# A streaming encoder layer whose product operands are laid out on 64-byte starts

## What is computed

```python
proj = rmsnorm(x) @ w_in                        # 1024 -> 4096: x_a | x_b | g_a | g_b
y_a  = rg_lru(causal_conv4(x_a))                # gates by 8 blocks of 128 x 128
y_b  = (pool(x_b) - x_b) @ w_g * scale          # 4 groups of 256, windows 2, 4, 8, 16
x = x + (sig(g_a) * (y_a @ w_br_a) + sig(g_b) * (y_b @ w_br_b)) @ w_out
gu = rmsnorm(x) @ w_gu                          # 1024 -> 2 x 2816
x = x + (silu(gu[:, :2816]) * gu[:, 2816:]) @ w_down
y = rmsnorm(x)                                  # final norm
```

## Time and profile before

| | |
|---|---|
| median of three runs | 2699.14 us |
| the profiled execution: its time | 2699.44 us |
| its span, first to last instruction | 2697.6 us |
| TensorE busy (matmul) | 2680.8 us, 15422 instructions |
| VectorE busy | 2053.7 us |
| ScalarE busy | 1359.4 us |
| GpSimd busy | 197.0 us |
| moved by DMA | 486.10 MB, mean 180 GB/s |

### The profile page before, as it was taken

The page is one execution under the profiler, slowest core; times in us unless marked ns, Lnnn a source line. Parts: engine busy times, 40 slices in busy tenths (PEclk is TensorE's granted clock), DMA queues, the critical chain, the costliest instruction groups (busy, mean ns, idle before and its releaser), DMA issues.

```text
span 2697.6 us, 39270 instructions
## 1 busy us (share of the span) xinstructions
PE 2680.8 (99%) x15422; PEld 2654.3 (98%) x15422; DVE 2053.7 (76%) x2737; ACT 1359.4 (50%) x1826; POOL 197.0 (7%) x369
## 2 busy tenths in 40 slices
PE   9999999999999999999999999999999999999998
PEld 7999999999999999999999999999999999999998
DVE  7868787888887878887677766688676779766677
ACT  6743584358445844583364444455343445444443
POOL 2000101020101010101010000001000000100000
PEclk9999999999999999999999999999999999999999
DMA  7453567546754676467465443456544454643434
GB/s 238 143 189 117 191 221 277 185 161 225 267 202 154 233 250 221 170 217 255 168 206 168 141 134 132 149 174 212 166 132 148 138 171 163 217 141 128 146 133 125
DMA packets 151318, 486.10 MB, mean 180 GB/s; under 512 B 16608, under 2 KB 36704, under 8 KB 151136
## 3 DMA queue, kind: packets, MB, share of 16 engines
q1 hardware_dynamic: 107808, 346.66, 38.0%
q0 software_dynamic: 33104, 121.92, 13.3%
q10 hardware_dynamic: 10224, 15.01, 1.6%
HBM read 419.01 MB, written 64.51 MB: 179 GB/s over the span
## 4 chain that ended last, share of the span: by engine, by line
PE 93%; DVE 3%; ACT 1%; DMA 1%; issue 1%; SPq 0%; DVEq 0%; ACTq 0%
PE ps L763 93%; DMA wraw<-dwm 1%; ACT wring L960 0%; DVE wring L1878 0%; DVE gb L1542 0%; DMA wraw<-graw 0%; DVE xacc L1923 0%; DVE wlast L1878 0%; SPq L534 0%; DVE xacc L1869 0%; ACT ycomb L1188 0%; DVE ycomb L1705 0%; DVE ga L2063 0%; DVE tot L1470 0%; DVE tmp L2061 0%
## 5 line engine op out<-in xcount | busy, mean ns | idle before, releaser
L763 PE MATMUL ps<-ycomb,wring 128*128 128x346 f32 (+1 forms) x5544 | 883.4, 321 | 0.3 <-DVE wring L1878 0.3
L763 PEld LDWEIGHTS ps<-ycomb,wring 128*128 128x128 f32 x5544 | 880.9, 188 | 0.6 <-DVE wring L1878 0.6
L1878 DVE TENSOR_TENSOR wring<-wraw,wring 128x1024 fp32r<-128x1024 f32 x527 | 642.4, 1220 | 251.9 <-ACT wring L960 249.2
L960 ACT ACTIVATE wring<-wraw 128x1024 fp32r<-128x1024 f32 x527 | 555.4, 1055 | 455.6 <-PE ps L763 418.8
L763 PE MATMUL ps<-xhi,wring 128*128 128x416 f32 (+1 forms) x1728 | 477.1, 353 | 2.3 <-DVE xlo L1971 2.3
L763 PE MATMUL ps<-yhi,wring 128*128 128x416 f32 x1568 | 429.2, 351 | 0.0
L763 PEld LDWEIGHTS ps<-xhi,wring 128*128 128x128 f32 x1728 | 325.2, 188 | 7.7 <-ACT xhi L1320 3.7
L763 PE MATMUL ps<-hcomb,wring 128*128 128x346 f32 (+1 forms) x2016 | 322.4, 321 | 0.0
L763 PEld LDWEIGHTS ps<-hcomb,wring 128*128 128x128 f32 x2016 | 320.8, 188 | 0.1
L763 PE MATMUL ps<-xlo,wring 128*128 128x416 f32 (+1 forms) x864 | 304.7, 353 | 0.0
L763 PEld LDWEIGHTS ps<-yhi,wring 128*128 128x128 f32 x1568 | 294.3, 188 | 1.9
(11 more groups left out here) (257 smaller groups left out, 2939.7 us busy)
## 6 DMA issues: line engine op xcount, KB each, us to landing
wraw<-dwm SPq DMA_DIRECT2D x247, 512.0 KB, 4.0
wraw<-sgu SPq DMA_DIRECT2D x132, 512.0 KB, 3.2
wraw<-graw SPq DMA_DIRECT2D x99, 512.0 KB, 3.5
wraw<-sdn SPq DMA_DIRECT2D x48, 512.0 KB, 3.5
pbuf<-graw POOLq DMA_DIRECT2D x22, 1024.0 KB, 7.1
sgu<-pbuf POOLq DMA_DIRECT2D x22, 1024.0 KB, 6.2
wraw<-fused SPq DMA_DIRECT2D x40, 512.0 KB, 3.2
wraw<-draw SPq DMA_DIRECT2D x36, 512.0 KB, 3.8
```

Of the source, the lines that this page charges most:

```text
L763: mm = nc.tensor.matmul(out, wt[:, c * P:(c + 1) * P], x, start=(first and q == 0), stop=(last and q == 2), skip_group_check=chain)
L960: A(ring(n)[:, 0, 0:c], raw_of(n)[:, 0:c], ACT.Copy, scale=cst[:, PSC, name[2]:name[2] + 1] if name[0] == "w" else 1.0).then_inc(w_hi, 1)
L1878: V.tensor_tensor(ring(n)[:, 1, 0:c], raw_of(n)[:, 0:c], ring(n)[:, 0, 0:c].bitcast(f32), SUB).then_inc(w_lo, 1)
```

## The change

The rows of feed-forward tiles get room for 352 columns in place of 348 (1408 bytes, 22 x 64). The region that holds the mixer's operands begins 32 bytes further on, and the regions behind it are moved along by what that and the wider rows need. The number of columns that are loaded, computed and stored stays TH.

```diff
--- before.py
+++ after.py
@@ -33,7 +33,7 @@
 NT = 3
 TH = (348, 346, 346)
 TO = (0, 696, 1388)
-HW = 348
+HW = 352
 PROD = (1, 2, 6, 5, 7, 3, 4)
 ROLE = {1: 0, 6: 0, 7: 0, 4: 0, 2: 1, 5: 2, 3: 2}
 OPENS = (1, 5, 2)
@@ -317,7 +317,7 @@
         xring = at(e0 + 14304, "xring", [P, XR, LW])
         work = at(e0, "work", [P, 15, HW])
 
-        a0 = e0 + 21216
+        a0 = e0 + 21248
         xhi, xlo = at(a0, "xhi", [P, KT, W], f32r), at(a0 + 13824, "xlo", [P, KT, W], f32r)
         yhi, ylo = at(a0 + 27648, "yhi", [P, KT, W], f32r), at(a0 + 41472, "ylo", [P, KT, W], f32r)
         sring, sraw = at(a0 + 55296, "sring", [P, 2, 2, 4 * P], f32r), at(a0 + 63488, "sraw", [P, 2, 4 * P])
@@ -326,22 +326,22 @@
         lac, fix = at(a0 + 76352, "lac", [P, 7, KT]), at(a0 + 76576, "fix", [P, 64])
         ycomb = at(a0, "ycomb", [P, 7, 2, 4, HW], f32r)
 
-        m0 = a0 + 77952
+        m0 = a0 + 78848
         mhi, mlo = at(m0, "mhi", [P, KT, LW], f32r), at(m0 + 13312, "mlo", [P, KT, LW], f32r)
         ga, gb = at(m0 + 26624, "ga", [P, KT, LW]), at(m0 + 39936, "gb", [P, KT, W])
         state = at(m0 + 53760, "state", [P, KT, NST])
         sums = at(m0 + 54976, "sums", [P, 2, LW], f32r)
-        main = at(m0 + 61248, "main", [P, KT, LW])
-        sq, tot = at(m0 + 74560, "sq", [P, 2, W]), at(m0 + 78016, "tot", [P, W])
-        rstd2 = at(m0 + 80736, "rstd_n2", [P, LW])
+        main = at(m0 + 61952, "main", [P, KT, LW])
+        sq, tot = at(m0 + 75264, "sq", [P, 2, W]), at(m0 + 78720, "tot", [P, W])
+        rstd2 = at(m0 + 80768, "rstd_n2", [P, LW])
         xres = at(m0, "xres", [P, KT, W])
         pbuf = at(m0, "pbuf", [P, 2, 4, 4 * P])
         wextra = at(m0 + 16384, "wextra", [P, 2, KT * P], f32r)
         xacc = at(m0, "xacc", [P, KT, 2 * HW])
-        hcomb = at(m0 + 22272, "hcomb", [P, 3, 2, 7, HW], f32r)
-        nsq, ntot = at(m0 + 61248, "nsq", [P, 2, 2 * HW]), at(m0 + 66816, "ntot", [P, 2 * HW])
-        tailsq, tailsum = at(a0, "tailsq", [P, 8, 2, HW]), at(a0 + 22272, "tailsum", [P, 2, 2, HW])
-        nrstd, nsum = at(m0 + 69600, "nrstd", [P, 2 * HW]), at(m0 + 72384, "nsum", [P, 2, 2 * HW], f32r)
+        hcomb = at(m0 + 22528, "hcomb", [P, 3, 2, 7, HW], f32r)
+        nsq, ntot = at(m0 + 61952, "nsq", [P, 2, 2 * HW]), at(m0 + 67584, "ntot", [P, 2 * HW])
+        tailsq, tailsum = at(a0, "tailsq", [P, 8, 2, HW]), at(a0 + 22528, "tailsum", [P, 2, 2, HW])
+        nrstd, nsum = at(m0 + 70400, "nrstd", [P, 2 * HW]), at(m0 + 73216, "nsum", [P, 2, 2 * HW], f32r)
         rstd = [rstd0, rstd1, rstd2]
         opnd = [(xhi, xlo), (yhi, ylo)]
         ps = ctx.enter_context(nc.psum_tensor("ps", [P, 8, 512], f32))
```

## The result

The changed kernel takes 2704.76 us (median of 11 runs, 2703.82 to 2706.77) where the kernel before takes 2699.14 (11 runs beside it, 2697.61 to 2700.44). The ratio is 1.0021 with a 95% interval of 1.0014 to 1.0029: slower by 5.6 us, at the edge of what can be told from no change, but clear of it. The forecast was 2696.

A forecast was written before the change was run, and what follows sets the result against it. TensorE was taken as the bound: the number of products times the distance between starts. Feed-forward -4 us plus mixer 0 gave -4 us on 2699.4, so 2695 to 2696, stated as 2696, counted as no change; range 2680 to 2712.

The forecast's parts named there:

- large gain: Rival, all products: the excess is a penalty for starts off multiples of 64; 228 us less, 2471 us; chance 0.04.
- the feed-forward's term: Feed-forward, 8316 products: -0.5 ns each, -4 us, within bounds of -19 to +19 us.
- a reason of pattern: Feed-forward: rows 1408 bytes apart alternate between two positions of 256 bytes, like mhi's, whose run has the smallest excess, 14.5 ns.
- The row it stood on: Feed-forward, one ycomb unit before the change: triples of four column blocks took 0.47, 0.48, 0.48, 0.48 us, the third aligned.
- The mixer's term: Mixer, 6768 products from xhi, xlo, yhi, ylo: 0 taken, within bounds of -8 to +31 us.
- The price of the rival: Mixer: the fusing block's difference between aligned and unaligned operands, up to +4.6 ns a product or +31 us.
- The prediction's own test: Fusing block: wextra's triples should go from 0.69 to 0.71 us if aligned starts are the slower ones.
- The rival that ended slower: Mixer: aligned moving operands meet aligned weight rows; up to +31 us (2730), half of it 2714; chance 0.16.
- The predicted small gain: Rival, everywhere: all streams fall to mhi's pace, -8 us in mixer and feed-forward each, 2683 to 2684; chance 0.32.
- the prediction's use of it: All products: by the skill's rule, columns / 2.4 + 2.5 ns, an estimated 2509 us if alignment were the fault.

## Why the prediction was wrong

**What held.** That only the distance between starts could move the time: the number of products is the same, TensorE stands at 99%, and VectorE, ScalarE and GpSimd are unchanged. That no large gain lay in alignment: aligned products pay an excess of 14 to 16 ns over their columns like any other.

**The step that failed** is the feed-forward's term, "I take -0.5 ns, for a reason of pattern", -4 us. It measured +4.5 us: gate-up products of 346 columns went up by 0.9 ns and down products by 1.3 ns, where both were to fall by 0.5. It failed in two ways. The row it stood on the earlier trace rows could tell a difference of 3 ns in a product; the bounds of -19 to +19 us were honest about it, the value between them was not supported. One unit was too little: averaged over the 308 such units (296 for the last block) of the same trace, the triples of j = 0, 1, 2, 3 cost 158.0, 159.2, 159.1 and 158.1 ns a product at 346 columns. The aligned one, j = 2, is 0.5 ns above the mean of the four, and j = 1, which is not aligned, as much: no sign of a gain by alignment, and a spread of 1.2 ns by place. And the pattern was read off one operand: mhi's pace of 187.8 ns at rows that step by 128 bytes belongs to that step together with its distance from the weights (32 bytes), not to the step alone. Moved to 192 bytes the same rows cost 188.9 ns, and ycomb with the same step costs 159.4 at 192, 160.7 at 160, 157.8 or 159.4 at 144.

**The mixer's term**, 0, measured +1.0 us, inside its bounds of -8 to +31. The price of the rival, 4.6 ns a product from the fusing block, was wrong: its two kinds of triples don't differ by alignment. The prediction's own test hints at it: wextra's triples went from 0.69 to 0.70 us where 0.71 was named, and wring's went down to 0.70 without being moved. The run with everything shifted shows it: with the alignments exchanged and the distances to sring kept, the triples cost what they cost before.

**The rival that ended slower** had the sign and spoke of the moving operand meeting "the same position as the weights being loaded beside it". That is close to what the runs show, but it was put in the mixer, where 1.0 of the 5.6 us fell, and it asked for equal positions as the slow ones. A product standing still has 159.5 ns at distance 0, 156.6 at 16 and 161.7 at 224; equal positions are neither the fastest nor the slowest. The predicted small gain was to be had, but from the shift alone (2.6 us); the wider rows took it back and more. The measured time lies inside the stated range, and that is no merit of the mechanism: the range reached up to 2712 for a loss in the mixer, and the loss came in the feed-forward.

TensorE: Matmul & The Clock Gate in the Trainium skill (Back-to-back issue gap) would have a product start columns / 2.4 + 2.5 ns after the last, 146.7 ns at 346 columns. The page gives this for an isolated matmul and says that in a stream where each matmul has its weight load both set the distance; this kernel is such a stream, so the prediction's use of it had the wrong case. No stretch of 346 columns in any run came under 156 ns, even with all other engines idle and the clock at 2.4 GHz; by the formula the kernel would take an estimated 190 us less. The same page (Step-by-step: what each phase is for) says that loading the next weights takes no read bandwidth from the matmul that runs, through a port of its own. The runs show that the places of the two operands don't act independently on the pace: moving the weights by 32 bytes alone moved ycomb's products from 159.4 to 160.7 ns. That the two reads collide inside SBUF is my reading of this and was not shown.

What stays open: which distances and row lengths are fast, as a rule. Most values repeat to 0.1 ns but follow no order that I found, and the second pace of one placement, and the mixer's two paces at the same addresses, say that a table of places is not enough.

## What to carry to other kernels

When TensorE is the bound and weights change with every product, the pace of a stretch depends on where its moving operand lies relative to its weights, modulo 256 bytes, by up to 2% at 346 columns in the kernel's order of operands (157.8 to 160.7 ns) and 3% standing still; an alignment of the moving operand to 64 bytes by itself was worth nothing here, and a change of layout that looks free can cost or gain some microseconds. Such a pace can be measured cheaply with products alone, since for the stretches compared it came out the same within about 0.2 ns without the rest of the kernel, but confirm it in the kernel, where a placement may settle at another pace. Here the best version found is the kernel before with the shift alone: 2696.86 us, 0.9990 of the time before (0.9981 to 0.9998).

## What was unexpected of the hardware

- A kernel moved as a whole by 32 bytes keeps every pace (108.84, 26.48 and 53.44 us for three stretches), while moving either operand alone by 32 bytes changes most of them.
- 346 columns can cost more than 348: 160.7 against 158.9 ns for gate-up products with the wider rows alone, 156.6 against 153.4 ns standing still at distance 16.
- One placement held 157.8 ns and 159.4 ns in turn in the same execution, for hundreds of products each, and one of the switches came at a single product delayed by 0.08 us.
